# RWKV block on one Trainium2 core: three weight loads are issued before the PP to PX copy, and one weight copy moves behind an exp pair

## What is computed

```python
r = xr @ w_r
w = -jax.nn.softplus(-(w0 + jnp.tanh(xw @ w1) @ w2)) - 0.5
k = xk @ w_k
v = xv @ w_v
a = jax.nn.sigmoid(a0 + (xa @ a1) @ a2)
g = jax.nn.sigmoid(xg @ g1) @ g2
...
decay = jnp.exp(-jnp.exp(heads(w)))
a_vec = -kk
b_vec = kk * a_h
...
state = state * w_t + sa * b_t + v_t * k_t     # one step per token, shortened
```

## Time and profile before

| what | value |
|---|---|
| median of 3 executions | 1371.91 us (1367.45 to 1374.14) |
| the profiled execution, its own time | 1370.58 us |
| its span in the trace | 1368.8 us |
| PE busy | 1340.3 us, 98% of the span |
| DVE, ACT, POOL busy | 862.4, 724.6, 187.4 us |
| granted TensorE clock | full in the whole span |

### The profile page before, as it was taken

The page is one execution under the profiler, slowest core; times in us unless marked ns, Lnnn a source line. Parts: engine busy times, 40 slices in busy tenths (PEclk is TensorE's granted clock), DMA queues, the critical chain, the costliest instruction groups (busy, mean ns, idle before and its releaser), DMA issues.

```text
span 1368.8 us, 24119 instructions
## 1 busy us (share of the span) xinstructions
PE 1340.3 (98%) x10262; PEld 1144.7 (84%) x10262; DVE 862.4 (63%) x1199; ACT 724.6 (53%) x1028; POOL 187.4 (14%) x179
## 2 busy tenths in 40 slices
PE   8999999999999999999999998999999999999999
PEld 8976989988898889988466877899998877799998
DVE  5657754557667655456798668655555678665554
ACT  5456654446654654445566554554454667654452
POOL 0263011000000011010131356000000134000000
PEclk9999999999999999999999999999999999999999
DMA  8634554665564555664547301555474532655472
GB/s 307 215 114 153 194 192 164 214 200 169 160 225 168 180 195 167 221 197 158 177 127 219 84 19 49 173 181 185 147 251 157 197 127 78 191 179 185 147 253 78
DMA packets 91519, 232.54 MB, mean 170 GB/s; under 512 B 20614, under 2 KB 26646, under 8 KB 91290
## 3 DMA queue, kind: packets, MB, share of 16 engines
q1 hardware_dynamic: 90840, 228.95, 51.7%
q0 software_dynamic: 576, 2.11, 0.5%
HBM read 227.87 MB, written 1.08 MB: 167 GB/s over the span
## 4 chain that ended last, share of the span: by engine, by line
PE 85%; DVE 6%; ACT 4%; DMA 2%; issue 1%; POOL 1%; SPq 1%; DVEq 0%; ACTq 0%; POOLq 0%
PE PS L459 82%; PE PS L462 4%; ACT SH L1296 1%; DVE SL L1746 1%; DMA ST<-in_w_attn_in 1%; DMA ST<-in_rw_w_v 1%; DVE XX L1740 1%; ACT JK L1293 1%; SPq L2672 1%; DVE SL L1740 1%; ACT AB L1293 0%; DVE X L1746 0%; POOL SM L2461 0%; DVE XL L1740 0%; ACT XT L1296 0%
## 5 line engine op out<-in xcount | busy, mean ns | idle before, releaser
L1746 DVE SCALAR_TENSOR_TENSOR SL<-ST,SM,SH 128x1024 fp32r<-128x1024 f32 (+1 forms) x256 | 315.5, 1255 | 155.1 <-ACT SH L1296 153.7
L1296 ACT ACTIVATE SH<-ST,SM 128x1024 fp32r<-128x1024 f32 (+1 forms) x256 | 281.7, 1121 | 177.1 <-PE PS L459 110.7
L459 PE MATMUL PS<-XH,SH 128*128 128x256 f32 x1224 | 343.6, 282 | 0.1
L459 PE MATMUL PS<-XH,SL 128*128 128x256 f32 x1224 | 343.2, 281 | 0.0
L459 PE MATMUL PS<-XL,SH 128*128 128x256 f32 x1224 | 342.3, 281 | 0.0
L1740 DVE TENSOR_TENSOR SL<-ST,SH 128x1024 fp32r<-128x1024 f32 (+1 forms) x153 | 192.9, 1276 | 142.4 <-ACT SH L1296 142.1
L1296 ACT ACTIVATE SH<-ST 128x1024 fp32r<-128x1024 f32 (+1 forms) x153 | 158.6, 1052 | 153.7 <-PE PS L459 124.6
L459 PEld LDWEIGHTS PS<-XH,SH 128*128 128x128 f32 x1224 | 231.4, 190 | 1.7 <-issue 0.7
L459 PEld LDWEIGHTS PS<-XL,SH 128*128 128x128 f32 x1224 | 228.6, 187 | 0.9
L459 PEld LDWEIGHTS PS<-XH,SL 128*128 128x128 f32 x1224 | 228.7, 187 | 0.2
L459 PE MATMUL PS<-SH,XH 128*128 128x512 f32 x544 | 220.8, 406 | 3.2 <-DVE SL L1740 1.6
(11 more groups left out here) (262 smaller groups left out, 1380.3 us busy)
## 6 DMA issues: line engine op xcount, KB each, us to landing
ST<-in_ffn_w_gu SPq DMA_DIRECT2D x80, 512.0 KB, 4.9
ST<-in_w_mlp_up SPq DMA_DIRECT2D x64, 512.0 KB, 5.2
ST<-in_w_mlp_down SPq DMA_DIRECT2D x64, 512.0 KB, 4.4
ST<-in_ffn_w_down SPq DMA_DIRECT2D x44, 512.0 KB, 4.4
ST<-in_w_attn_in SPq DMA_DIRECT2D x24, 512.0 KB, 5.0
ST<-in_w_conv_in SPq DMA_DIRECT2D x24, 512.0 KB, 4.5
ST<-in_w_ple_gate SPq DMA_DIRECT2D x16, 512.0 KB, 3.6
ST<-in_kv_w SPq DMA_DIRECT2D x16, 512.0 KB, 3.5
```

The costliest lines, as they stand in the source:

```text
L459: return e.matmul(o, l, r, start=start, stop=stop, skip_group_check=True)
L1296: return e.activation(o, x, ACT.Copy, **kw)
L1746: return e.scalar_tensor_tensor(o, x, a, y, op, op2)
```

## The change

Two edits. On ACT, `rounded(234)` inside the loop over m becomes `rounded(233 + m)`: the copy of unit 232 stays between the two exp pairs, and that of unit 233 comes behind the second pair. On SP, `loads(241)` is put between the stores to `scr2` and the wait for PE's last r unit, so units 238, 239 and 240 are issued before the copy to PX.

```diff
@@ -1558,7 +1558,7 @@
         w.wait_ge(*at("cumsum", m))
         act(M.PI[:, m, :], pair(4 + 2 * m), ACT.Exp, scale=EM05)
         act(M.PP[:, m, :], pair(4 + 2 * m), ACT.Exp, scale=-EM05).then_inc(*inc("pp", m))
-        rounded(234)
+        rounded(233 + m)
     rounded(235)
     w.wait_ge(*at("tk"))
     for m in range(2):
@@ -2746,6 +2746,7 @@
     w.wait_ge(*at("pp", 1))
     for m in range(2):
         load("scr2", (), M.scr2[2 * m:2 * m + 2, :], M.PP[63:128:64, m, :])
+    loads(241)
     w.wait_ge(*U.result(at, "rr", 1))
     for c in range(2):
         load("px", (), M.PX[64 * c + 1:64 * c + 64, :, :], M.PP[64 * c:64 * c + 63, :, :])
```

## The result

The changed kernel is slower: 1376.48 us in the median (1374.45 to 1377.72) against 1371.91, a ratio of 1.0034 with an interval of 1.0025 to 1.0044, so +4.6 us. That is within the 0.5% called "same" above, but outside the predicted range and of the other sign.

A forecast was written before the change was run, and what follows sets the result against it. PE bounds the kernel, busy 1340.3 of 1368.8 us. Gaps of 0.78 and 0.67 us go, and 0.67 of the 0.97: 2.12 us, so 1371.9 - 2.1 = 1369.8 us, range 1365.5 to 1373.5.

The forecast's parts named there:

- same: Whole kernel: the time stays within 0.5%, 6.9 us, of before; chance 0.93, with faster 0.04 and slower 0.03.
- The ceiling: PE, 715 to 760 us: three gaps of 0.78, 0.67 and 0.97 us, sum 2.42 us, the most the edits can give.
- ACT's edit: Before the first g1 matmul: PE's gap waiting for the second PP goes whole, 0.78 us, bounds 0 and 0.78.
- 3.4 us of cover: Unit 237: its load, issued later at 721.7, lands at 725.7, and ACT copies it only at 729.15.
- The loads: Units 238 to 240, issued ahead of PX: land in 3.9 us plus half a us; the 0.67 us gap goes.
- The PX copy: SP's queue before KK times PX: transfer 8.4 us from 729, landing at 737.4, early 733.9, late 740.2.
- the sum: KK times PX to unit 240: 737.4 + 5.67 = 743.07 instead of 745.19, a gain of 2.12 us.
- The figure of nine engines: PX copy: 63 rows go over 9 of 16 DMA engines; at the page's 261 GB/s it would take 4.0 us.
- The sign: Whole kernel: a gain of 2.1 us, median from 1371.9 to 1369.8 us; this forecast case had chance 0.58.
- PX late: Rival at the PX copy: lands at 740.2 or later, unit 240 at 745.9, 0.7 us lost, 1372.6; chance 0.13.
- late bound: PX landing: start at 729.7, plus 9.5 us of transfer and 1 us for completion, 740.2.

The follow-up runs named there:

- b6_no_px: Changed kernel without the PX copy, DVE multiplying KK with PP instead and nobody waiting for PX: 1368.40 us against 1369.70 for the kernel before, ratio 0.9988.
- a1_act_only: Kernel before with only ACT's edit, the copy of unit 233 behind the second exp pair, SP's order unchanged: 1373.02 us against 1370.02, ratio 1.0018.
- b3: Changed kernel with SP waiting for PX to land before issuing units 241 to 243: 1371.56 us against 1369.70 for the kernel before, ratio 1.0005.
- d4: Kernel before with SP waiting for PX to land before it issues unit 238: executed once, 1372.96 us.
- b5_warm7: Changed kernel with 7 idle matmuls on PE ahead of unit 240: 1377.47 us against 1369.70 for the kernel before, ratio 1.0047.
- d1: c1 with row R_LW later, SP waiting for PX before the row and units 244 on, and DVE copying VN earlier: ratio 1.0011 to the kernel before.
- d3: d1 without ACT's edit (units 232 and 233 both between the exp pairs): ratio 1.0025 to the kernel before.
- e1: d1 with ACT's VN copy ahead of its copies of units 244 to 246: ratio 1.0014 to the kernel before.
- c1: Changed kernel with loads to 243 ahead of PX, their low parts ahead of KK times PX, DVE's VN before low parts of 244 to 246: ratio 1.0028 to before.
- b1: Kernel before with each PX copy of 63 rows issued as pieces of 48 and 15 rows: ratio 0.9996.
- c2_row_later_act: Kernel before with ACT's edit and row R_LW moved from ahead of PX to behind unit 243: ratio 1.0009.
- c4_low_first_row: c1 with row R_LW moved behind the PX copy as well: ratio 1.0029 to the kernel before.
- d2_changed_again: Changed kernel run once more, unchanged, for a second trace: 1376.23 us against 1371.54 for the kernel before, ratio 1.0040.

## Why the prediction was wrong

- **The ceiling** (2.42 us of gaps): nearly right. In b6_no_px no gap is left from g1 to the scan, and the transposes start at 753.20 instead of 756.41, 3.2 us earlier: a gap costs a little more than its length, for the first matmuls behind it start 0.34 us apart and not 0.23. As a bound for the whole effect it misled, because it says nothing about the other side, and I let it set the range.
- **ACT's edit**, "worth 0.78 us": the gap goes, at 720.99, but the step "3.4 us of cover" failed. I counted the cover of unit 237's own use and not what stands behind 237 in SP's queue; a1_act_only measured +1.8 us for PX and +2.1 for unit 238. In before's SP order it costs 2.5 to 3 us.
- **The loads**: unit 238 lands in 3.7 us and the gap at 238 goes, as forecast; this was what the edit does. 239 and 240 took 6.5 and 8.5 us, not 3.9 and half a us more, so PX's first packet was started at 730.75, not at 729: 1.75 us of the miss. (the earlier trace rows names the PX copy, but its landings are those of 238 and 239 only; no row gives that of PX.)
- **The PX copy**, the step on which the sum stood: forecast to land at 737.4, landed at 744.1. The mechanism of the sum was right (744.29 + 5.67 = 749.96, measured 749.98); the term was mis-sized. The miss of 6.7 us is 1.75 us of a later start and 4.95 us of a longer transfer: 13.35 us from 730.75 where I took 8.4, from one us of the trace at 123 GB/s. The rate was not the fault, since alone the copy took 7.6 us (b3) and 8.9 us (d4). The overlap was: I took the time of a copy by itself for one that three loads run beside, and without them (b3) nearly all of the loss was gone. I had named these loads in the rival, with 241 alone and 0.7 us, and had not drawn the consequence of my own step: low parts of 238 and 239 at 734.8 release 242 and 243 some 4.7 us earlier than before, right into the copy.
- **The clock**: not in the prediction at all. A wait of 7.57 us is priced at 1.5 us more; b5_warm7 shows that it is the clock.
- **The figure of nine engines**: the trace's share of 0.55 agreed with the Trainium skill, DMA: Bandwidth & Descriptors, section "Why a DMA increments its semaphore by 16 and not by 1", by which 63 rows are spread over nine engines. The 27 GiB/s an engine of its Specifications give, as an estimate, 4.0 us for the copy. The traces differ: 7.6 and 8.9 us even alone, and the measurement decides. Splitting the rows over more engines raised the share to 0.92 and not the rate, and changed nothing in the median that can be measured (0.9996, 0.9987 to 1.0006).
- **The sign**: the rival "PX late" had the place and the direction, and 0.13. Its price of 0.7 us was a tenth of the 6.15 us in the trace, since its late bound was built from the same early start and from the mixed stretch of the earlier trace rows. There, also among loads, PX's last packet was started 8.3 us behind its first (724.60 and 732.91); in the changed kernel it was 12.1 us (730.75 and 742.81). Why loads beside it slowed it more here than before isn't shown. The class, within 0.5%, came out by luck: 4.6 us is inside 6.9, but with the other sign, and the argument for it was the ceiling of a gain.

## What to carry to other kernels

A transfer that is moved back in a queue is not only later by what is ahead of it. What the reordering makes early releases further transfers, and these run beside it: follow each freed buffer to the load that it lets go. Price a landing in two parts, the time until the first packet and the time from there, and take the second from a stretch with as much traffic beside it as there will be: here the same copy took 7.6 us alone and 13.4 beside three loads. And ask of each delayed load what stands behind it in the same queue.

A gap of the busiest engine is worth its length only if the next wait moves with it. In a1_act_only PE's head start of 0.78 us was waited off at the next load, and the longer wait brought a lower clock on top.

## What the runs showed of the hardware

- The SBUF to SBUF copy of 2 x 63 rows of 8 KB, 1.03 MB, takes 10.8 us from issue to landing with nothing issued behind it (d4), 11 to 13 us with more loads ahead of it and none behind (b3, d1, d3, e1), and 13.1 to 17.6 us with loads of 512 KB beside it (c1 to the changed kernel). From its first packet to its landing it is 7.6 to 10 us without and 10.2 to 13.4 us with loads beside it, in the eleven traces that show its landing for 63 rows in one piece.
- Of the same copy, 63 rows in one piece kept 0.56 of the 16 DMA engines busy and moved 168 GB/s, pieces of 48 and 15 rows kept 0.92 busy and moved 160 GB/s (d4 and b1, 727 to 729 us).
- After waits of PE of 7.57, 5.50, 3.82, 3.14, 2.04 (d4_px_bare) and 1.76 us (c2_row_later_act) the granted clock fell to about 0.50 for a few us, part of it in the following work; after others of 1.98 (b3_px_alone) and 2.57 us (c4_low_first_row) it did not. So the length of the wait alone did not decide it. It also falls in places that have nothing to do with the change, and not in every execution. In d2_changed_again it fell near the start, in three stretches of 2 us:

```profile
28.00:30.00 2.00, 0.81 (x7) 0.84 (x8) 1.33 (x4) 1.15 (x1) 0.00 (x0) 1.00 0.98 363
30.00:32.00 2.00, 2.00 (x12) 2.00 (x12) 1.52 (x2) 0.00 (x0) 0.00 (x0) 0.52 0.95 356
32.00:34.00 2.00, 2.00 (x13) 2.00 (x13) 0.00 (x0) 0.00 (x0) 0.00 (x0) 0.63 0.86 311
```

The 3.3 us of work at 0.50 above cost 1.5 us, so such a stretch can be a part of the scatter between executions of one kernel; how large a part isn't shown.
